# Second products of the feed-forwards: two products of 256 tokens in place of one of 512

## What is computed

```python
D_FF = 2816
def swiglu(h, w_in, w_out):
    gate, up = jnp.split(h @ w_in, 2, axis=-1)
    return (jax.nn.silu(gate) * up) @ w_out
```

## Time and profile before

| what | value |
|---|---|
| median of 3 runs | 3452.98 us (3449.61 to 3456.88) |
| profiled execution, span | 3443.2 us; it has no other time of its own |
| mean granted TensorE clock | 0.966 |
| PE (matmul) busy | 3301.5 us, 96% |
| DVE, ACT, POOL busy | 61%, 34%, 39% |
| matmuls and weight loads | 16010 each |

### The profile page before, as it was taken

The page is one execution under the profiler, slowest core; times in us unless marked ns, Lnnn a source line. Parts: engine busy times, 40 slices in busy tenths (PEclk is TensorE's granted clock), DMA queues, the critical chain, the costliest instruction groups (busy, mean ns, idle before and its releaser), DMA issues.

```text
span 3443.2 us, 43632 instructions
## 1 busy us (share of the span) xinstructions
PE 3301.5 (96%) x16010; PEld 2594.6 (75%) x16010; DVE 2088.4 (61%) x2758; ACT 1178.2 (34%) x1800; POOL 1343.7 (39%) x565
## 2 busy tenths in 40 slices
PE   8999999999996999899998999989998999989998
PEld 6657787657775888787777888878887877778886
DVE  3877785877775445997277543464469944684422
ACT  3354323355323223333243222332233324332223
POOL 3302342302333445444043545634464421534454
PEclk9999999999998999999799999999999998999999
DMA  4524472523553332566132332323236861423322
GB/s 135 171 78 129 141 230 77 162 80 123 155 172 97 97 89 88 93 110 116 46 110 74 104 97 82 106 86 96 83 92 84 128 95 41 132 80 97 94 81 75
DMA packets 589027, 363.70 MB, mean 106 GB/s; under 512 B 58178, under 2 KB 538828, under 8 KB 588620
## 3 DMA queue, kind: packets, MB, share of 16 engines
q1 hardware_dynamic: 585044, 355.21, 39.5%
q10 hardware_dynamic: 3832, 6.42, 0.5%
HBM read 346.63 MB, written 12.58 MB: 104 GB/s over the span
## 4 chain that ended last, share of the span: by engine, by line
PE 57%; DVE 6%; DMA 2%; SPq 1%; ACT 1%; POOL 1%; issue 1%; ACTq 0%; POOLq 0%; DVEq 0%
PE bank L158 17%; PE bank L160 17%; PE bank L159 17%; DMA w_raw<-in_mix_w_in_dram 2%; SPq L1722 1%; PE bank L2009 1%; PE bank L2008 1%; POOL w_lo L152 1%; DVE xT L2443 1%; DVE w_s L2328 1%; PE bank L2030 1%; PE bank L2018 1%; PE bank L2010 1%; PE bank L1992 0%; DVE y_s L2431 0%
## 5 line engine op out<-in xcount | busy, mean ns | idle before, releaser
L152 POOL TENSOR_TENSOR w_lo<-w_raw,w_hi 128x1024 fp32r<-128x1024 f32 (+2 forms) x552 | 1335.7, 2425 | 2063.1 <-ACT w_hi L144 2063.1
L158 PE MATMUL bank<-xh,w_lo 128*128 128x512 f32 x2432 | 980.4, 403 | 47.1 <-DVE xl L2408 28.2
L160 PE MATMUL bank<-xh,w_hi 128*128 128x512 f32 x2432 | 969.1, 398 | 0.0
L159 PE MATMUL bank<-xl,w_hi 128*128 128x512 f32 x2432 | 964.4, 397 | 0.0
L144 ACT ACTIVATE w_hi<-w_raw 128x1024 fp32r<-128x1024 f32 (+2 forms) x552 | 565.9, 1028 | 785.3 <-PE bank L160 686.6
L158 PEld LDWEIGHTS bank<-xh,w_lo 128*128 128x128 f32 x2432 | 465.3, 191 | 166.2 <-issue 46.9
L159 PEld LDWEIGHTS bank<-xl,w_hi 128*128 128x128 f32 x2432 | 465.7, 191 | 106.3 <-issue 4.3
L160 PEld LDWEIGHTS bank<-xh,w_hi 128*128 128x128 f32 x2432 | 465.1, 191 | 101.4
L160 PE MATMUL bank<-HH_s,w_hi 128*128 128x512 f32 x704 | 276.1, 392 | 0.0
L159 PE MATMUL bank<-HL_s,w_hi 128*128 128x512 f32 x704 | 275.6, 391 | 0.0
L158 PE MATMUL bank<-HH_s,w_lo 128*128 128x512 f32 x704 | 275.2, 391 | 0.0
(11 more groups left out here) (506 smaller groups left out, 4511.4 us busy)
## 6 DMA issues: line engine op xcount, KB each, us to landing
w_raw<-in_ffn_w_in_dram SPq DMA_DIRECT2D x176, 512.0 KB, 3.8
m_raw_l<-in_mod_w_dram SPq DMA_DIRECT2D x128, 512.0 KB, 4.8
w_raw<-in_w_in_dram SPq DMA_DIRECT2D x80, 512.0 KB, 3.8
w_raw<-in_mix_w_in_dram SPq DMA_DIRECT2D x64, 512.0 KB, 9.5
w_raw<-in_ffn_w_out_dram SPq DMA_DIRECT2D x64, 384.0 KB, 3.5
w_raw<-in_ffn_w_out_dram SPq DMA_DIRECT2D x64, 320.0 KB, 3.2
m_half_l<-in_mod_w_dram SPq DMA_DIRECT2D x32, 256.0 KB, 2.7
w_raw<-in_w_out_dram SPq DMA_DIRECT2D x16, 512.0 KB, 4.3
```

The lines of the kernel that those rows point to most:

```text
L152: nc.gpsimd.tensor_tensor(ring.lo[s][:, 0:width], ring.raw[s][:, 0:width], ring.hi[s][:, 0:width].bitcast(F32), ALU.subtract).then_inc(rin ...
L158: nc.tensor.matmul(out, wl, xh, start=start, stop=False)
L159: nc.tensor.matmul(out, wh, xl, start=False, stop=False)
L160: return nc.tensor.matmul(out, wh, xh, start=False, stop=stop)
```

## The change

A second form of `mm3` is added, and only the second products of the feed-forwards use it. For the first 256 tokens and then for the last 256 it issues the three matmuls, each into its half of the bank. The flag that starts a bank is set on the first matmul of the first half alone, and the flag that ends it on the last of the second half. `product` is given a parameter that selects the form; all its other callers keep `mm3`. The signal to the ring stays on the last matmul that `product` issues.

```diff
+def mm3_halves(nc, out, wh, wl, xh, xl, start, stop):
+
+    for t in (slice(0, T // 2), slice(T // 2, T)):
+        nc.tensor.matmul(out[:, t], wl, xh[:, t], start=start and t.start == 0, stop=False)
+        nc.tensor.matmul(out[:, t], wh, xl[:, t], start=False, stop=False)
+        last = nc.tensor.matmul(out[:, t], wh, xh[:, t], start=False, stop=stop and t.stop == T)
+    return last
@@ product
-        def product(out, n, b, kt, x, x_lo, wait=None, off=0, k0=0, total=None, at=0):
+        def product(out, n, b, kt, x, x_lo, wait=None, off=0, k0=0, total=None, at=0, three=mm3):
@@
-                last = mm3(nc, out, wh[:, cc], wl[:, cc], x[:, k0 + k, :], x_lo[:, k0 + k, :],
-                           k0 + k == 0, k0 + k == total - 1)
+                last = three(nc, out, wh[:, cc], wl[:, cc], x[:, k0 + k, :], x_lo[:, k0 + k, :],
+                             k0 + k == 0, k0 + k == total - 1)
@@ ffn, second product
-                    product(bank[m % 2], n, b, CUT[b + 1] - CUT[b], HH, HL, k0=CUT[b], total=FT).then_inc(ring.used, 1)
+                    product(bank[m % 2], n, b, CUT[b + 1] - CUT[b], HH, HL, k0=CUT[b], total=FT, three=mm3_halves).then_inc(ring.used, 1)
```

## The result

The changed kernel takes 3467.6 us (median of 8 runs, 3460.53 to 3472.15), the kernel before 3451.74 us (median of 8, 3445.95 to 3459.37). The ratio is 1.0045, 95% interval 1.0035 to 1.0055: slower by 12 to 19 us. The forecast was 3461.7 us, slower. The profiled execution spans 3458.6 us, 15.4 more than before; its time of 3460.53 us is the lowest of the eight.

What follows compares the result with a forecast made beforehand. TensorE's sequence of products was taken as the bound. Span 3443.2 us, plus 8.7 for 2112 pairs at 4.1 ns each, plus 9.8 between span and median, gave 3461.7 us; range 3449 to 3490.

Steps and rivals of the forecast that it cites:

- TensorE's sequence of products is the whole bound in the four stages: In the four feed-forward stages only TensorE's products set the length; each nanosecond added to a product shows in the end.
- 2112 x (2p - 228.9): Cost of splitting 2112 second products of 228.9 ns into pairs, p being the distance at 256 tokens: +8.7 us.
- p = 116.5 ns: Distance between successive 256-token second products: 115.7 ns of stream plus 0.8, so each pair costs 4.1 ns more.
- the stream: Time one 256-token second product needs for its tokens: 2.4 ns fixed plus 113.3, together 115.7 ns.
- the closeness of the load: 0.8 ns added per 256-token product, for the load's 112 ns lying near the stream's 115.7 and line 1995's higher slope.
- The excess grows with the tokens: The second products' excess over one clock a token grows with width; line 1995 gave 0.47 ns a token, not 0.417.
- rival with 15.6 ns fixed: All 15.6 ns fixed per second product: p 122.3 ns, +33 us, 3486; chance 0.25 together with a partial clash.
- A load allows 112 ns a product and hides under a longer stream: In the second products, one weight load each allows p = 112 ns and no less, 4 ns under the stream's 115.7.
- rival in which the load shows: Second products wait for their load's record: p 190.4 ns, +321 us, 3774; chance of a fully exposed load 0.04.
- Faster, the load is the only limit: Second products' stream needs 109 ns, so the load's 112 decides: -10 us, 3443; chance 0.09 including balanced out.
- 9.8 us between span and median, carried over: The kernel before had a profiled span 9.8 us below its median run; the forecast time adds the same 9.8.
- Nothing beside it costs: Ring helpers, VectorE, instruction fetch, and drain and eviction at a bank's end were said to add nothing.

Runs made afterwards that it cites:

- second profile: The changed kernel run again with no edit: 3467.4 us, span 3465.5 us.
- three profiles whose second products are halves throughout: The changed kernel, the same unaltered again, and a version with each weight tile's two halves next to each other: 3467.6 (median), 3467.4 and 3463.56 us.
- runs with 64 columns: Second products with 64 weight columns instead of 128, at 512, 256 and 128 tokens: 3447.62, 3467.4 and 3479.7 us, against 3453.6 for the kernel before.
- 64-column quarters: Second products written as four products of 128 tokens with 64 weight columns instead of 128: 3479.7 us, against 3453.6 for the kernel before.
- quarters: Second products written as four products of 128 tokens with full weights: 3916.23 us, against 3448.96 for the kernel before.
- uneven cut: Second products written as 384 and 128 tokens instead of two halves: 3565.94 us, against 3448.96 for the kernel before.

## Why the prediction was right, and by how much it was off

- *TensorE's sequence of products is the whole bound in the four stages:* right. No stage has more wait in it than before, the clock stayed at 1.00, and what a product gained in distance the stage gained in time.
- *2112 more matmuls and loads, 2112 x (2p - 228.9):* right as a sum. With p = 117.78 the term is +14.1 us and the second profile's stages grew by 14.2.
- *p = 116.5 ns:* this is the mis-sized term. It is 117.78 where a stage is slow, as it was behind 9 of the 12 stage entries in the three profiles whose second products are halves throughout; 2 of the 3 quick ones turned slow after some 70 steps. The pair costs +6.7 ns, not +4.1, and that is the difference between the forecast +8.7 us and +14.1. The medians differ by 15.9, just above the forecast's band of +5 to +15. Its first part, the stream, was taken at 2.4 + 113.3 = 115.7. The runs with 64 columns give 116.7, so what is fixed per product is 3 to 5 ns and not the 2.4 of the transposes. Its second part, 0.8 for the closeness of the load, is 1.1 against the stream alone. Both were small errors to the same side, doubled by the pair.
- *The excess grows with the tokens:* right, and line 1995 was the row to trust. Per token it is 0.44 and the reading of 0.47 with an error of 0.03 held it. The rival with 15.6 ns fixed would have made the 64-column quarters 68.9 ns; they are 60.0.
- *A load allows 112 ns a product and hides under a longer stream:* right. The quarters had 111.7 and the uneven cut +117 us as worked out. The rival in which the load shows is refuted by the same two runs. The rule of the Trainium skill (TensorE: Matmul & The Clock Gate, "The mechanism") that a load overlaps a matmul only when the row group differs does not hold here either: halves on the same rows have a load and a stream in each 117.8 ns.
- *Faster, the load is the only limit:* wrong as a whole, but not empty. One stage in four had 113.3 ns, 1.6 above the load's limit and below the point of 114.45 from which a pair gains. I had named a stall that a short stream does not meet; what it is instead is one of two regular patterns of load and stream.
- *All stages alike:* implied by one value of p, and wrong. It fails a test that the prediction itself set ("if a stage grows by over 4 us or shrinks"): three stages grew by 3.6 us, but the last one of the first profile shrank by 1.0. That p has two values was no term of the sum, and that most stages fell on the dearer one, 1.3 ns from the forecast, is part of why the forecast was near.
- *9.8 us between span and median, carried over:* near in size (9.0 in the changed kernel), and partly luck. In each run of the changed kernel the time is some 2 us over its span. The rest is that both first profiles happened to be of low runs; the second profile's run took 3467.4 us, the median.
- *The Trainium skill's gap of N/2.4 + 2.5 ns* (TensorE: Matmul & The Clock Gate, "Back-to-back issue gap"): the fixed part is near what the 64-column runs show, but the rate per token is not, 116.7 and 228.3 ns where it gives 109 and 216. Its +5.3 us for the whole change was further off than the forecast's +8.7.
- *Nothing beside it costs:* right as far as the stages go. The 5.6 us outside them in the first profile are within what the same code differs by between profiles.

## What to carry to other kernels

A product of fp32r tokens costs the longer of its stream and one weight load. Here that is about 0.44 ns a token and 3 to 5 ns for the one, 112 ns for 128 fp32 columns for the other. So with full weights a cut into 256 and 256 tokens was nearly free (+14 us for 2112 of them), and one that left a part of 128 was ruinous (+117 and +467 us). Price a cut from the distances between record starts, never from record durations (0.28 against 0.39 us here), and look first for a row of the same type with another width. Where stream and load come out nearly equal, expect the distance to differ from stage to stage and from run to run, and take a second profile before explaining one stage by what is in it.

## What the runs showed of the hardware that was not expected

- With 128 weight columns and 256 fp32r tokens the steps settle at 117.78 or 113.33 ns, each without a break for up to 1055 products in a stage and for thousands where all products are in halves. With all products in halves there is a third value near 120, mostly in the first block.
- Which of the two follows can be told from the last 512-token record: 11 of 11 after a duration of 394 ns (a step of 231 or 232) were quick, 41 of 41 after 388, 392 or 397 slow. Why was not found. It is not the only way in: with all products in halves there is no such record, and stretches of 616 and 1990 quick steps (from 1780 and 1930 us) began behind a 256-token step of 221 ns. A transpose ended each of the three quick stretches of second products that met one.
- With 64 columns neither value appears, at 116.7. At 128 tokens there are again two means, 60.0 and 62.2, the second from a transpose to the end of one stage.
- Steps of 512 tokens go round in a cycle of 226, 229 and 232 ns (now and then 225, 230 and 231) with a mean of 228.9 between transposes in all four stages, whether VectorE is busy for 88 us of the stage or for 16.
